# A two-layer decoder trunk on one core: first retention output weights loaded ahead of the rows, the first norm's second root moved forward, and the attention items placed three products later

## The chip, the cores and the metric

One NeuronCore of a Trainium2 chip runs the whole program. The metric is the device time of one execution in microseconds (us). TensorE does the matrix products; VectorE (DVE), ScalarE (ACT) and GpSimd (POOL) prepare its operands and take its results out of PSUM; SyncE (SP) issues nearly all transfers. The engines run their own instruction streams in a fixed order and meet at semaphores only.

## What is computed

The trunk has two pre-norm layers on 1024 tokens of width 1024, in float32. Layer 0 mixes by multi-scale retention, layer 1 by a gated linear recurrence; each is followed by a SwiGLU feed-forward part (hidden width 2816), and a last RMSNorm ends it. The change lies in the first norm and in the retention of layer 0:

```python
h = rms_norm(x, mix_norm[0])
q, k, v, g = split(h @ w_in)          # 1024, 1024, 2048, 2048 columns
q, k = rope(q), rope(k) * dk ** -0.5  # 4 heads of 256
scores = (q_i @ k_i.T) * decay        # chunk by chunk, a running state beside it
o = scores @ v_i + (q_i @ state) * q_decay
state = state * chunk_decay + (k_i * k_decay).T @ v_i
x = x + (rms(o) * silu(g)) @ w_out
```

## The kernel before, in words

**Products.** Every float32 operand is held as a high and a low part, and one product of 128x128 by 128x512 is three TensorE instructions (`three`, L1197: high by high at L1199, high by low at L1202 and L1203). The input projection runs in 24 units (`IN_ORDER`), each with a 2x2-block scheme of PRODUCTS = 7 products, so a product has a number j = 7r + p, with unit r and place p from 0 to 6; each is 4 calls of `three`, 12 instructions. Every product needs its own 128x512 weight form: ACT rounds it (L1895, in the first two units L1915), POOL takes the rest (`f_lo_of`, L927), and POOL also makes the sums of weight blocks (`f_add`, L930). ACT rounds the form of product j + 3 after product j.

**Start.** Units 0 and 1 run interleaved, while the first norm is still being made. The norm has two halves of 512 tokens. For the second half ACT and DVE square the rows, DVE sums the squares (L2543), ACT takes the root (L1822), DVE the reciprocal (L2545), both scale the rows (ACT L1987, DVE L2645), TensorE turns them (L1347), and DVE and ACT form sums and high and low parts (L2662, L2673, L1960, L1965) for the products of units 0 and 1. In ACT's program (`norm_by_halves_act`, L1949, `scaled_last`, L1990) this root stands behind four copies out of PSUM (`plain`), one weight form (`unit(3)`) and one copy of a product (`first_term`, L1923). In POOL's program (`first_units`, L961) six weight sums stand together between the fourth and the fifth weight form.

**Rotations.** Units 4, 5, 6, 7, 10, 11, 14 and 15 give q or k, which DVE rotates in twelve 128x512 operations (`turned`, L2822, at L2836): 1 and 2 at p = 4 (they read PSUM), 3 to 6 at p = 5, 7 to 9 at p = 6, 10 to 12 at p = 0 of the next unit. Operations 3 to 12 read two SBUF operands.

**Items.** The attention is cut into 16 items (4 heads by 4 pieces of 256 tokens), each with four parts that all engines put behind the same product: part 0 turns the keys and takes the scores (`keys_and_scores`, TensorE at L1578; ACT and DVE `item_keys`, with DVE's L2868, L2871, L2873), part 1 turns the values (L1598), part 2 gives outputs and state, part 3 turns the outputs back (L1632), and ACT rounds and DVE lowers the next item's q and k (ACT L2147, L2148; DVE `item_lower`, L2861, L2863). The table `PARTS` puts part m = 4 it + part behind product 47 + 16m // 9, so part 0 of item 0 is behind p = 5 of unit 6, and the last part behind p = 5 of unit 22. TensorE's part 0 waits for `item_lower` (item 0's stands behind product FIRST_PART - 1), its part 1 for DVE's `item_keys`.

**The end of the projection.** Then `out_rows` multiplies the gated rows by `w_out`: 64 weight units w, eight for the first head's rows in each half. SP's order there is: store of item 15 (L656), `load_rows(0)`, `(1)`, `(2)` (L673, two transfers of 1 MB each), the spill of unit 22 (L600, four of 256 KB), out weights 0 to 3 (L583), 4 to 7, the spill of unit 23, `load_rows(3)`. DVE gates the rows (`rows_gated`, L2903), ACT rounds them (`rows_upper`, L2194), DVE lowers them (`rows_lower`, L2907); ACT rounds the out weights (L2207) and POOL lowers them (L1143). ACT's `in_first_quarter` (L2131) of unit 23 waits for the spill of unit 22, since it writes what that spill reads.

## Time and profile before

| what | us |
|---|---|
| median of 3 runs | 2639.61 (2639.51 to 2641.33) |
| profiled execution, its own time | 2641.87 |
| its span | 2640.0 |
| TensorE busy | 2574.9 (98%) |
| GpSimd busy | 1701.5 (64%) |
| VectorE busy | 1486.8 (56%) |
| ScalarE busy | 1056.0 (40%) |
| granted TensorE clock, mean | 0.994 |

The busy time of an engine is the union of its instructions' durations. A row of the timeline gives start, duration, engine, line, operation and tiles, and in brackets how long the engine had been idle and what released it.

### The profile page before, as it was taken

The page shows a single profiled execution, that of the slowest core. Times are in us where ns is not written, and L with a number is a line of the kernel's source. Part 1 is how long each engine was busy: PE and PEld are TensorE (multiplying, and loading weights), DVE is VectorE, ACT ScalarE, POOL GpSimd, SP SyncE. Part 2 cuts the span into 40 slices and gives each one's busy share as a digit, 9 for nine tenths or more (in the row PEclk, how much of TensorE's full clock was granted, in tenths as well). Part 3 has the DMA queues.
Part 4 walks back from the last instruction along what each step waited for, and adds up shares of the span by engine and source line. Part 5 has one row for each costly group of instructions (what it writes and reads, how often), then busy time and mean ns, then how long its engine had stood idle before and what let it go on. Part 6 is the DMA issues. An engine that isn't in the chain of part 4 may idle for free.

```text
span 2640.0 us, 34384 instructions
## 1 busy us (share of the span) xinstructions
PE 2574.9 (98%) x11625; PEld 2118.0 (80%) x11625; DVE 1486.8 (56%) x1762; ACT 1056.0 (40%) x1753; POOL 1701.5 (64%) x1277
## 2 busy tenths in 40 slices
PE   6999999999999999999999999999999999999998
PEld 5778887888788788888888788888877888888887
DVE  8685647343341856556463738365688464655644
ACT  6333343555344533333333614324256333333324
POOL 5864555455565488878788645263454788887865
PEclk9999999999999999999999999999999999999999
DMA  3433533344852121121212011111111112112122
GB/s 114 138 104 115 157 120 112 112 144 145 301 191 80 49 61 52 48 60 42 61 59 64 29 49 50 39 54 40 41 56 49 48 48 64 48 48 64 48 68 84
DMA packets 250796, 214.85 MB, mean 81 GB/s; under 512 B 12481, under 2 KB 204225, under 8 KB 250689
## 3 DMA queue, kind: packets, MB, share of 16 engines
q1 hardware_dynamic: 250464, 213.40, 25.6%
q8 instruction: 62, 1.02, 0.2%
q14 instruction: 46, 0.37, 0.0%
q10 hardware_dynamic: 224, 0.07, 0.0%
HBM read 175.67 MB, written 37.75 MB: 81 GB/s over the span
## 4 chain that ended last, share of the span: by engine, by line
PE 80%; DVE 11%; issue 4%; ACT 3%; DMA 1%; POOL 1%; SPq 0%; DVEq 0%; ACTq 0%; POOLq 0%
PE ps L1199 26%; PE ps L1203 26%; PE ps L1202 26%; DVE residual L3135 2%; DVE f_h_lo L2673 1%; DVE uc L3229 1%; DVE gate_buf L2836 1%; PE ps L1347 1%; DVE uc L3223 1%; PE ps L1598 1%; DVE rope_part L2836 0%; DVE gate_buf L3234 0%; DMA projected<-gate_buf 0%; PE ps L1632 0%; DVE f_h_lo L2662 0%
## 5 line engine op out<-in xcount | busy, mean ns | idle before, releaser
L927 POOL TENSOR_TENSOR f_w_lo<-f_raw,f_w_hi 128x512 fp32r<-128x512 f32 x406 | 577.4, 1426 | 384.3 <-ACT f_w_hi L1895 221.6
L1199 PE MATMUL ps<-f_h_hi,f_w_hi 128*128 128x512 f32 x1904 | 749.4, 394 | 10.8 <-POOL f_w_lo L927 4.6
L1203 PE MATMUL ps<-f_h_hi,f_w_lo 128*128 128x512 f32 x1904 | 743.6, 391 | 0.0
L1202 PE MATMUL ps<-f_h_lo,f_w_hi 128*128 128x512 f32 x1904 | 743.0, 390 | 0.0
L1199 PEld LDWEIGHTS ps<-f_h_hi,f_w_hi 128*128 128x128 f32 x1904 | 359.0, 189 | 93.9 <-issue 9.4
L927 POOL TENSOR_TENSOR f_w_lo<-f_sum,f_w_hi 128x512 fp32r<-128x512 f32 x210 | 316.0, 1505 | 182.0 <-ACT f_w_hi L1895 181.3
L1203 PEld LDWEIGHTS ps<-f_h_hi,f_w_lo 128*128 128x128 f32 x1904 | 358.4, 188 | 75.7
L1202 PEld LDWEIGHTS ps<-f_h_lo,f_w_hi 128*128 128x128 f32 x1904 | 359.1, 189 | 71.8
L1895 ACT ACTIVATE f_w_hi<-f_raw 128x512 fp32r<-128x512 f32 x248 | 156.5, 631 | 400.6 <-PE ps L1203 396.0
L1199 PE MATMUL ps<-f_w_hi,f_act_hi 128*128 128x512 f32 x616 | 240.8, 391 | 4.5 <-DVE residual L3135 4.5
L1202 PE MATMUL ps<-f_w_lo,f_act_hi 128*128 128x512 f32 x616 | 239.8, 389 | 0.0
L1203 PE MATMUL ps<-f_w_hi,f_act_lo 128*128 128x512 f32 x616 | 239.7, 389 | 0.0
L3135 DVE TENSOR_TENSOR residual<-ps,residual 128x512 f32<-128x512 f32 x316 | 205.6, 684 | 54.4 <-PE ps L1203 54.4
L1895 ACT ACTIVATE f_w_hi<-f_sum 128x512 fp32r<-128x512 f32 x186 | 117.1, 630 | 234.0 <-PE ps L1203 230.1
L3023 DVE TENSOR_TENSOR gate_buf<-ps,gate_buf 128x512 f32<-128x512 f32 x120 | 82.9, 691 | 210.4 <-PE ps L1203 210.3
L900 POOL TENSOR_TENSOR small<-w_raw 128x1 f32<-128x1 f32 x72 | 26.2, 364 | 242.5 <-PE ps L1199 242.5
L930 POOL TENSOR_TENSOR f_sum<-f_sum,f_raw 128x512 f32<-128x512 f32 x124 | 182.0, 1468 | 0.0
L1143 POOL TENSOR_TENSOR ret_out_lo<-f_raw,ret_out_hi 128x512 fp32r<-128x512 f32 x64 | 101.8, 1595 | 84.5 <-ACT ret_out_hi L2207 84.5
L1199 PE MATMUL ps<-h_hi,w_hi 128*128 128x512 f32 x384 | 151.3, 394 | 1.0 <-DVE h_lo L2565 0.6
L1203 PE MATMUL ps<-h_hi,w_lo 128*128 128x512 f32 x384 | 149.5, 389 | 0.0
L1202 PE MATMUL ps<-h_lo,w_hi 128*128 128x512 f32 x384 | 149.5, 389 | 0.0
L1199 PEld LDWEIGHTS ps<-f_w_hi,f_act_hi 128*128 128x128 f32 x616 | 115.6, 188 | 32.4 <-DVE residual L3135 8.2
(343 smaller groups left out, 4564.7 us busy)
## 6 DMA issues: line engine op xcount, KB each, us to landing
f_raw<-in_ffn_w_gu SPq DMA_DIRECT2D x176, 256.0 KB, 3.6
f_raw<-in_ret_w_in SPq DMA_DIRECT2D x96, 256.0 KB, 5.0
projected<-gate_buf SPq DMA_DIRECT2D x96, 256.0 KB, 4.2
f_raw<-in_ffn_w_down SPq DMA_DIRECT2D x88, 256.0 KB, 2.8
f_raw<-in_ret_w_out SPq DMA_DIRECT2D x64, 256.0 KB, 3.3
w_raw<-in_lru_w_in SPq DMA_DIRECT2D x48, 256.0 KB, 2.9
residual<-in_x SPq DMA_DIRECT2D x16, 512.0 KB, 6.9
v_raw<-projected SPq DMA_DIRECT2D x16, 512.0 KB, 3.8
```

Of the source, the lines that this page charges most:

```text
L927: nc.gpsimd.tensor_tensor(lo, src, hi.bitcast(F32), ALU.subtract).then_inc(f_wready, 1)
L930: nc.gpsimd.tensor_tensor(out, one, other, op).then_inc(f_summed, 1)
L1143: nc.gpsimd.tensor_tensor(lo_, f_in_raw(w % 8), hi.bitcast(F32), ALU.subtract).then_inc(f_wready, 1)
L1199: m = nc.tensor.matmul(o, l_hi, r_hi, start=start, stop=False, skip_group_check=onto)
L1202: nc.tensor.matmul(o, l_hi, r_lo, start=False, stop=False, skip_group_check=onto)
L1203: return nc.tensor.matmul(o, l_lo, r_hi, start=False, stop=stop, skip_group_check=onto)
L1347: m = nc.tensor.transpose(ps[:, b * BANK + s * P:b * BANK + (s + 1) * P], xn_at(half, hf * 4 + s)[:, k * P:(k + 1) * P], ident[:])
L1598: m = nc.tensor.transpose(bank(4 + blk, d * P, P), v_raw[:, d * ITEM + blk * P:d * ITEM + (blk + 1) * P], ident[:])
L1895: nc.scalar.activation(f_unit(j)[0], src, ACT.Copy).then_inc(f_whi, 1)
L2673: TT(H_lo[:, h_cut(form, k)], src[:, t_cut(k)], H_hi[:, h_cut(form, k)].bitcast(F32), ALU.subtract).then_inc(hn_dve, 1)
L3023: TT(t, f_bank(u, p), t, ALU.add).then_inc(f_ev, 1)
L3135: TT(X[:, c], ps[:, b * BANK:(b + 1) * BANK], X[:, c], ALU.add).then_inc(f_ev, 1)
```

## The change

There are four parts; the diff keeps every changed line.

1. **Transfers at the end of the projection.** SP loads out weights 0 to 3 ahead of `load_rows(0)`; `load_rows(1)` follows the spill of unit 22, and `load_rows(2)` the spill of unit 23. DVE gates rows 0 at p = 2 of unit 23 and lowers them at p = 4, ACT rounds them at p = 3 and rounds out weights 0 and 1 ahead of its copy at p = 4. Rows 1 are gated, rounded and lowered only in the output stage, ahead of out weight 4.
2. **First norm.** ACT does one of the four copies ahead of the second root, `unit(3)` between root and scaling, and `first_term` and the other three copies between the two halves of the scaling. DVE makes three low parts (L2662) ahead of four squares.
3. **POOL's first sums.** The six sums are spread between the weight forms in pairs, two of them ahead of the fourth form.
4. **Items.** Part m goes behind product 50 + 7m // 4. This puts the parts 0, 1, 2, 3 behind p = 1, 2, 4, 6 of every unit from 7 to 22. Rotation operations 5 and 6 stand behind an item's part at p = 5, where there is one.

```diff
 ITEM_PARTS = 4
-FIRST_PART = 47
+FIRST_PART = 50
 PARTS = {}
 for m in range(ITEM_PARTS * ITEMS):
-    PARTS.setdefault(FIRST_PART + m * 16 // 9, []).append((m // ITEM_PARTS, m % ITEM_PARTS))
+    PARTS.setdefault(FIRST_PART + m * 7 // 4, []).append((m // ITEM_PARTS, m % ITEM_PARTS))
 def chunks_before(it):
...
 ROWS_IN = (0, 1, 2, 0, 1, 0, 1, 0)
-ROWS_AT = {8: 2, 14: 3, 20: 4, 24: 5, 28: 6, 35: 7}
+ROWS_AT = {4: 1, 8: 2, 14: 3, 20: 4, 24: 5, 28: 6, 35: 7}
 END_0 = counts(1, GROUPS_OF_4[0])
...
 SUMS_FIRST = [(0, 1), (0, 2), (0, 3), (1, 1), (1, 2), (1, 3), (0, 6), (1, 6)]
+SUMS_RET = [(u, p) for p in (1, 2, 3, 6) for u in range(2)]
...
+def first_sums(n, u, p):
...
+    return n.sums + (SUMS_RET if n == NOTHING else SUMS_FIRST).index((u, p)) + 1
...
                         if r == IN_UNITS - 2 and p == 6:
-                            load_rows(0)
-                            load_rows(1)
-                            load_rows(2)
-                        if r == IN_UNITS - 1 and p == 3:
                             for w in range(4):
                                 out_weight(w)
+                            load_rows(0)
+                        if r == IN_UNITS - 1 and p == 3:
+                            load_rows(1)
                 for w in range(4, 8):
...
                 spill(IN_UNITS - 1)
+                load_rows(2)
                 load_rows(3)
...
                     if w in (18, 24, 30, 33):
...
                 n = FIRST[layer]
-                units, sums = n.units, n.sums
+                units = n.units
                 raws = [[f_in_raw(4 * u + i) for i in range(4)] for u in range(2)]
                 def landed(u, i):
...
                 def summed(u, p):
-                    pool.wait_ge(f_summed, sums + SUMS_FIRST.index((u, p)) + 1)
+                    pool.wait_ge(f_summed, first_sums(n, u, p))
...
                     landed(u, 1)
...
                     lower(0, 4, raws[0][3])
+                    sum_1(0)
+                    sum_1(1)
                     landed(1, 3)
                     lower(1, 4, raws[1][3])
-                    for u in range(2):
-                        sum_1(u)
-                        sum_3(u)
-                        sum_2(u)
-                    sum_4(0)
                     lower(0, 1, f_in_sum(0))
                     lower(1, 1, f_in_sum(1))
-                    sum_4(1)
+                    sum_3(0)
+                    sum_3(1)
                     lower(0, 2, raws[0][1])
                     lower(1, 2, raws[1][1])
-                    summed(0, 3)
+                    sum_2(0)
+                    sum_2(1)
                     lower(0, 3, raws[0][0])
-                    summed(1, 3)
                     lower(1, 3, raws[1][0])
+                    sum_4(0)
+                    sum_4(1)
                     lower(0, 5, raws[0][2])
...
                     lower(0, 6, raws[0][3])
...
                 else:
-                    act.wait_ge(f_summed, n.sums + SUMS_FIRST.index((u, p)) + 1)
+                    act.wait_ge(f_summed, first_sums(n, u, p))
                 src = f_in_sum(u) if p == 1 else f_in_raw(slot)
...
-                def scaled_last():
+                def scaled_last(amid=lambda half: None):
                     root(4, SB, turn_b)
+                    amid(0)
                     act.wait_ge(n_rstd, turn_b)
                     for half in range(2):
+                        if half:
+                            amid(1)
                         scaled(6, half)
...
                         square_rows(s, 0, t_b[:, t_cut(s - 4)])
-                    for k in FOUR:
-                        plain(4 + k)
-                    unit(3)
-                    first_term(c, 1, AT_FIRST)
-                    scaled_last()
+                    plain(4)
...
+                    def between(half):
+                        if half == 0:
+                            unit(3)
+                        else:
+                            first_term(c, 1, AT_FIRST)
+                            for k in (1, 2, 3):
+                                plain(4 + k)
+                    scaled_last(between)
+                    unit(4)
                     act.wait_ge(n_sq, SB)
...
                     q_12(0)
...
                 from_sum(H_T1, 3, t_a, "T1")
-                unit(4)
+                if layer != RET:
+                    unit(4)
                 q_12(3)
...
                 for k in FOUR:
...
                             turn_table(p - 2, (sin_t, cos_t)[p - 2])
+                        if j == PROJECTED - 3:
+                            out_round(0)
+                            out_round(1)
                         if p == 4 and kind in "vg":
...
                         if p == 5 and kind == "g":
...
                                     item_rounded(it + 1)
-                        if r == IN_UNITS - 1:
-                            if p == 3:
-                                rows_upper(0)
-                            elif p == 4:
-                                out_round(0)
-                                out_round(1)
-                            elif p == 5:
-                                rows_upper(1)
+                        if j == PROJECTED - 4:
+                            rows_upper(0)
                 out_round(2)
             def out_ahead(end, done=[3]):
...
                         plain(H_Q11, k, k, "Q11h")
+                    for k in (0, 1, 2):
+                        plain(H_Q21, k, 4 + k, "Q21h")
                     square(5)
...
                     square(7)
-                    for k in FOUR:
-                        plain(H_Q21, k, 4 + k, "Q21h")
+                    plain(H_Q21, 3, 7, "Q21h")
                 else:
...
                         adds(0, 0)
...
                     dve.wait_ge(f_mm, PRODUCTS * r + 5)
-                elif first == 2:
+                elif first < 6:
                     dve.wait_ge(f_ev, in_ev(r, E_C21))
...
                     dve.wait_ge(f_ev, in_ev(r, E_C12))
...
                             if turn:
-                                turned(r, 2, 6)
+                                turned(r, 2, 4)
                         elif p == 6:
...
                         turn_arguments(r, p)
...
                                 item_lower(it + 1)
+                        if p == 5 and turn:
+                            turned(r, 4, 6)
                         if p == 6 and turn:
...
                         if r == IN_UNITS - 1:
-                            if p in (2, 3):
-                                rows_gated(p - 2)
-                            elif p == 5:
+                            if p == 2:
+                                rows_gated(0)
+                            elif p == 4:
                                 rows_lower(0)
-                rows_lower(1)
             def out_rows():
-                for q in range(2, 7):
+                for q in range(1, 7):
                     rows_gated(q)
...
                 for nh in range(2):
```

## Rows read from the trace of the kernel before

**Rows 1.** Page, busy time of TensorE (us, share, instructions)

```profile
PE 2574.9 (98%) x11625; PEld 2118.0 (80%) x11625; DVE 1486.8 (56%) x1762; ACT 1056.0 (40%) x1753; POOL 1701.5 (64%) x1277
```

**Rows 2.** TensorE's waits: total us, times, longest us

```profile
PE ps L1598 <- DVE item_kt_lo L2871: 4.3, 2, 2.2
...
PE ps L1578 <- DVE item_k_lo L2863: 4.3, 2, 3.3
...
PE ps L1199 <- DVE item_k_lo L2863: 1.0, 1, 1.0
```

**Rows 3.** Stretches: busy us of each engine, clock, DMA share, GB/s

```profile
26.40:66.00 39.60, 32.92 (x143) 25.88 (x142) 37.10 (x48) 24.77 (x45) 27.82 (x19) 0.91 0.04 10
...
168.00:182.00 14.00, 10.68 (x46) 9.09 (x45) 8.64 (x12) 4.55 (x8) 5.67 (x5) 0.76 0.61 185
...
661.00:666.00 5.00, 5.00 (x24) 4.14 (x23) 2.14 (x1) 0.00 (x0) 0.00 (x0) 1.00 1.05 390
```

**Rows 4.** Timeline of ACT, first norm

```profile
24.53 2.47 ACT L1960 ACTIVATE gate_buf<-ps,cols 128x512 f32<-128x512 f32 x4
...
27.81 0.38 ACT L1822 ACTIVATE rstd<-ssq,small 128x4 f32<-128x4 f32 x1
```

**Rows 5.** Timeline of DVE, first norm

```profile
25.11 0.15 DVE L2543 TENSOR_TENSOR ssq<-ssq 128x4 f32<-128x4 f32 x1
...
33.38 2.71 DVE L2662 SCALAR_TENSOR_TENSOR h_sum_a<-ps,cols,h_q 128x512 f32<-128x512 f32 x4
```

**Rows 6.** Timeline of TensorE, first norm

```profile
30.87 0.30 PE L1347 MATMUL ps<-ident,f_xn 128*128 128x128 f32 x1 [3.67 <-DVE f_xn L2645]
...
41.24 0.50 PE L1199 MATMUL ps<-f_h_hi,f_w_hi 128*128 128x512 f32 x1 [2.33 <-POOL f_w_lo L927]
```

**Rows 7.** Timeline of TensorE, items

```profile
172.37 0.45 PE L1578 MATMUL ps<-ident,k_raw 128*128 128x128 f32 x1 [3.32 <-DVE item_k_lo L2863]
...
209.82 0.45 PE L1598 MATMUL ps<-ident,v_raw 128*128 128x128 f32 x1 [2.15 <-DVE item_kt_lo L2871]
...
294.31 0.60 PE L1578 MATMUL ps<-ident,k_raw 128*128 128x128 f32 x4
...
296.13 0.40 PE L1199 MATMUL ps<-f_h_hi,f_w_hi 128*128 128x512 f32 x1
...
301.60 0.60 PE L1598 MATMUL ps<-ident,v_raw 128*128 128x128 f32 x4
```

**Rows 8.** Timeline of DVE, unit 5's rotation (no item in it), and one of POOL beside it

```profile
149.57 0.69 DVE L2806 TENSOR_TENSOR gate_buf<-gate_buf,ps 128x512 f32<-128x512 f32 x1 [1.33 <-PE ps L1203]
...
150.29 1.82 DVE L2836 TENSOR_TENSOR rope_part<-gate_buf,sin 128x512 f32<-128x512 f32 x1
...
157.14 0.68 DVE L2806 TENSOR_TENSOR gate_buf<-gate_buf,ps 128x512 f32<-128x512 f32 x1
...
158.84 1.77 DVE L2836 TENSOR_TENSOR gate_buf<-gate_buf,sin 128x512 f32<-128x512 f32 x1
...
161.13 0.68 DVE L2836 TENSOR_TENSOR gate_buf<-gate_buf,cos 128x512 f32<-128x512 f32 x1
...
150.28 1.29 POOL L927 TENSOR_TENSOR f_w_lo<-f_sum,f_w_hi 128x512 fp32r<-128x512 f32 x1 [0.17 <-ACT f_w_hi L1895]
```

**Rows 9.** Timeline of TensorE, first out weight

```profile
672.81 0.79 PE L1199 MATMUL ps<-ret_out_hi,rows_hi 128*128 128x512 f32 x1 [6.28 <-POOL ret_out_lo L1143]
```

**Rows 10.** Timeline of ACT and SP, end of the projection

```profile
658.94 1.91 ACT L2194 ACTIVATE rows_hi<-rows_o 128x2048 fp32r<-128x2048 f32 x1
...
668.69 0.60 ACT L2131 ACTIVATE gate_buf<-ps 128x512 f32<-128x512 f32 x1 [7.84 <-DMA projected<-gate_buf]
...
646.04 0.37 SPq L656 DMA_DIRECT2D attended<-o_raw  x1
```

**Rows 11.** Timeline of DVE, end of the projection

```profile
656.29 2.28 DVE L2903 TENSOR_TENSOR rows_o<-rows_o,rows_g 128x2048 f32<-128x2048 f32 x1
...
669.34 2.29 DVE L2907 TENSOR_TENSOR rows_lo<-rows_o,rows_hi 128x2048 fp32r<-128x2048 f32 x1
```

## The prediction

> **What bounds the kernel now.** I read the page first: TensorE is busy for 2574.9 of 2640.0 us [rows 1], so a gain can only be idle time of TensorE, 65 us, or time at its lower clock. Next, TensorE's waits [rows 2]: the reader should see that two of DVE's item steps, L2863 and L2871, hold it for 9.6 us. The timeline then places the waits. There are three places that the change touches: the first norm (idle 3.67 us ahead of 30.87 and 2.33 us ahead of 41.24 [rows 6]), the items (3.32 and 2.15 us [rows 7], one of 2.2 and two of 1.0, the rest of [rows 2]), and the first out weight (6.28 us [rows 9]). Last the stretches, for the clock: 0.91 in 26.4 to 66 and 0.76 in 168 to 182 [rows 3], a mean over the two levels of 1.2 and 2.4 GHz. In 168 to 182 the time lost is 14 x 0.24 = 3.4 us, of which I take 3.1 as lost by work. The second part of the idle time thus costs nearly as much as the first.
>
> **Sizes used below.** Two products fill the time from 296.13 to 301.60, so one is 2.73 us; part 0 of an item is 296.13 - 294.31 = 1.82 us [rows 7]. Parts 1 and 3, eight turns each, are two such sets of four, some 0.85 us each (0.6 us pipelined for four [rows 7]).
>
> **Part 1, the end of the projection: 7.3 us gained.** What is late now is a transfer. After the store of item 15 at 646.04 [rows 10] SP issues 6 MB of rows and then the 1 MB spill of unit 22; with the 0.5 MB store that is 7.86 million bytes, at 390 GB/s [rows 3] 20.2 us and some 2 us of latency: 668.2. The trace has ACT's copy behind that spill at 668.69, after 7.84 us of waiting [rows 10], and the out weights are rounded behind the copy. TensorE starts at 672.81 [rows 9]. In the new order I count from E, the end of the last product. Item 15 ends one product later, behind (22, 6), so its store goes out at about E - 17.4 (seven products are 19.1 us; ACT's copies follow the turns by some 1.7). Ahead of rows 0 there are then 0.5 + 1 MB, and 2 MB are theirs: 3.67 million bytes, 9.4 + 2 us, E - 6. DVE gates them in 2.28 us [rows 11] to E - 3.7, ACT rounds them in 1.91 us [rows 10] to E - 1.8, then two out weights (0.6 each) to E - 0.6. The spill has landed at E - 3.3 and is no longer waited for. DVE lowers the rows in 2.29 us [rows 11] to E + 0.6. So 0.6 us of idle time is left, up to 1.5 where a DVE operation meets one of POOL's; I take 1.0. Gone are 5.3 us of idle time, and the low clock behind it: 672.81 began at half speed, for which I take 2.0 us (4.3 us at half speed costs about 2). Moved past on SP: rows 1 now land at E + 1 or 2 with 6.5 MB ahead, needed through out weight 8 at E + 22; out weight 8 has 12.75 MB ahead of it, 34.3 us, and lands at E + 19, covered by out weights 0 to 7. Without that cover it would cost 1 to 3 us. Bounds: 4.3 gained (rows_gated and rows_lower each 1.1 longer, the spill late) to 8.3.
>
> **Parts 2 and 3, the first norm: 4.3 us gained.** The root stands at 27.81, while its sum is there at 25.26 [rows 4, 5]. With one copy ahead (four take 2.47 us, from 24.53 [rows 4]) ACT is free at 25.15, and the root is at 25.35: 2.5 us earlier. DVE's three low parts are only moved ahead of the squares: the same number stands ahead of the sum. The first set of turns follows, but the last three copies are now behind the first half of the scaling, and DVE's first sum waits for the last copy: I get 29.9 in place of 33.38 [rows 5], by seven operations of 0.6 (a weight form, two scalings, `first_term`, three copies) from 25.7 on. That is 3.5 us, and from there DVE is the bound, busy for 37.10 of 39.60 us [rows 3]. POOL's spread sums free its port in 33 to 38, where they double the length of DVE's operations; it gives 2 us to DVE and takes over half back later, since two sums then stand ahead of the weights of products (0, 3) and (1, 3). I take 0.8 of it. Lower bound 2.5 (the root alone); upper 7.5, which is the idle time of [rows 6] with half of the clock's 3.6 us. Unit 2's weights are loaded behind these, so the gain is carried on.
>
> **Part 4, the items: 8.0 us lost.** The title says three products later, and the count is 50 + 7m // 4: part 0 always behind p = 1. There is never a part at p = 5, so moving rotations 5 and 6 changes no order at all: it costs nothing and gives nothing. What counts is how much of DVE's work stands between the product (r, 5), time 0, and the part that TensorE wants. Unit 5 shows it without an item [rows 8]: operation 3 at 0.72, C12 (the third combination) at 7.57, operation 8 at 9.27, operation 10 at 11.56. An operation with two SBUF operands takes 1.7 us from start to start beside POOL and 0.6 without (operations 3 and 10: 1.82 and 0.68 long).
> - *Item 0.* `item_lower(0)` now stands behind operations 3 to 9 of unit 6, so its two steps start at 11.56 and end at 12.8; POOL is idle by then, as TensorE is held. TensorE wants them after three products, at 8.2. It idles for 4.7 us where it idled for 3.32 [rows 7]. With the same 3.1 us of clock that is 7.8 against 6.4.
> - *Units 7, 10, 11, 14, 15,* rotated with the next item behind. To TensorE's part 0 there are 2.73 x 3 + 0.85 = 9.1 us; to its part 1, 13.6. DVE has C21, operations 3 to 6, C12, two lowering steps, operations 7 to 12, one sum, the mask and the keys' low part: 10.5 us alone. Up to 7.57 the rows show four operations met by POOL (4 x 1.1 = 4.4 us), and after it I take one partly (0.4) and one fully (1.1): 16.4. So TensorE idles for 2.8 us each time, in two pieces, 14.0 in all. With none met by POOL it would be 0, with all of them 5.
> - *Gone:* 6.4 (item 0), 2.15 [rows 7] with an estimated 1.5 of clock (between none and the 3.1 of item 0), 2.2 and two of 1.0 [rows 2]: 14.3 in all.
> Loss: 7.8 + 14.0 + 0.5 for clock - 14.3 = 8.0. The other ten units have no rotation, and their lowering steps end by 8.3, ahead of 9.1.
>
> One rule is weighed here. [Rows 8] give 1.7 us for the operation that meets POOL, a cost of 1.1 over its 0.6, and I use that. The Trainium skill, page "SBUF — State Buffer", section "Who interferes with whom", says that a DVE instruction with two SBUF inputs and a GpSimd instruction that reads SBUF take the shared port in turn, and that the one that comes second is blocked for the whole of the other. By that rule each of the 5.4 meetings of a unit would cost a whole POOL instruction, 1.29 us [rows 8], 0.19 more, and the sum would be 5 us later, near 2641.
>
> **Sum.** -7.3 - 4.3 + 8.0 = -3.6 us. Against the profiled execution (2641.87 with 1.87 around its span of 2640.0) that gives 2638.3; the median of the runs is 2.3 lower, and I put the sum against it: 2639.6 - 3.6 = 2636.0.
>
> **Rivals.**
> - *The rotations collide less, clearly faster.* POOL's forms follow ACT, and ACT stands behind item work in half of these units; where POOL pauses, operations 5 and 6 fall to 0.6 us. With 1.2 us per unit in place of 2.8, part 4 costs nothing, and the time is 2628. For it: in units with an item at p = 5 these two operations do run at 0.6. Against it: that pause came from the item being there, and now there is none. With gains of part 1 and 2 at their upper ends it is 2627.
> - *DVE becomes the bound at the items, slower.* One mechanism: the lowering steps and the keys' low part come 5 us late in all five units (every operation met by POOL), 25 us in place of 14, each pause long enough to drop the clock as at 172.37. Then part 4 costs 19 us and more, and the sum is 2647. It decides from 4.6 us per unit. Against it: POOL has six instructions in that time, not ten.
> - *The transfers hold the first out weight as before.* If rows 0 were not in by E - 2, part 1 gives 3 and not 7: 2640, no change.
>
> **How the numbers follow.** A measurement of this kernel can tell about 0.2% (5.3 us) from no change: faster is below 2634.3, slower above 2644.9. The forecast, with part 4 between 6 and 13 us, has 0.35, the third rival (with the rule's 2641) 0.08: no change 0.43. The first rival has 0.30, and the upper ends of parts 1 to 3 with my part 4 have 0.12: faster 0.42, high because the sum stands only 1.7 us from that bound. The second rival has 0.15. The range takes in the first rival and goes four fifths of the way from the forecast to the second: 2627 to 2645.
>
> **What would show it.** Right: the root at about 25.4, DVE's first sum at 30, the first out weight within 2 us of the last product, a wait of some 4.7 us for L2863 at the first item, and waits for L2863 and L2871 in the units after 7, 10, 11, 14 and 15. Wrong: TensorE's waits for L2863 and L2871 below 12 us in total (then it is faster), or above 25 us (slower), or ACT still waiting for the spill ahead of L2131.

## The result, and the profile after

The changed kernel takes 2644.45 us (median of 17 runs, 2641.12 to 2648.64), the kernel before 2640.31 in the same comparison (17 runs, 2638.66 to 2642.68). The ratio is 1.0016, 95% interval 1.0010 to 1.0023: 4.2 us slower, between 2.6 and 6.1. That is within the 0.2% called "no change" in the prediction, and just inside its range, but it lies on the other side of 2639.6 than the 2636.0 forecast. The profiled execution took 2644.24, with a span of 2642.4.

TensorE's waits in the changed kernel (total us, times, longest), the rows that answer to [rows 2]:

```profile
PE ps L1585 <- DVE item_k_lo L2878: 10.4, 6, 4.8
...
PE ps L1605 <- DVE item_kt_lo L2886: 8.1, 5, 1.6
...
PE ps L1206 <- POOL ret_out_lo L1150: 3.8, 2, 3.5
```

The reader is to see 18.5 us of item waits where there were 9.6, and 3.5 ahead of the first out weight where there were 6.28 [rows 9]. Lines are shifted by some 7 in PE's part and some 15 in DVE's: L1585 is the old L1578, L2878 the old L2863. The timeline of TensorE places them; its first row answers to the first of [rows 7], its last to [rows 9]:

```profile
181.39 1.08 PE L1585 MATMUL ps<-ident,k_raw 128*128 128x128 f32 x4 [4.84 <-DVE item_k_lo L2878]
...
212.21 0.63 PE L1585 MATMUL ps<-ident,k_raw 128*128 128x128 f32 x4 [1.11 <-DVE item_k_lo L2878]
...
218.56 1.06 PE L1605 MATMUL ps<-ident,v_raw 128*128 128x128 f32 x8 [1.61 <-DVE item_kt_lo L2886]
...
675.92 0.50 PE L1206 MATMUL ps<-ret_out_hi,rows_hi 128*128 128x512 f32 x1 [3.48 <-POOL ret_out_lo L1150]
```

The pair 1.11 + 1.61 = 2.72 us stands five times, for the rotations of units 7, 10, 11, 14 and 15. The last product of the projection ends at 672.44 (666.53 before), so the first out weight stands 3.1 us later than before in all.

In the first norm, these rows of ACT and DVE answer to [rows 4, 5]:

```profile
26.28 0.30 ACT L1829 ACTIVATE rstd<-ssq,small 128x4 f32<-128x4 f32 x1 [0.76 <-DVE ssq L2557]
```

```profile
26.10 0.15 DVE L2557 TENSOR_TENSOR ssq<-ssq 128x4 f32<-128x4 f32 x1
...
30.57 2.73 DVE L2676 SCALAR_TENSOR_TENSOR h_sum_a<-ps,cols,h_q 128x512 f32<-128x512 f32 x4 [0.98 <-ACT gate_buf L1967]
...
46.08 6.80 DVE L2687 TENSOR_TENSOR f_h_lo<-h_sum_a,f_h_hi 128x512 fp32r<-128x512 f32 x4
...
53.47 2.81 DVE L2701 TENSOR_TENSOR h_sum_a<-h_sum_a,gate_buf 128x512 f32<-128x512 f32 x2
...
61.14 0.69 DVE L2687 TENSOR_TENSOR f_h_lo<-h_sum_a,f_h_hi 128x512 fp32r<-128x512 f32 x1 [0.17 <-ACT f_h_hi L1972]
```

The root is 1.5 us sooner and DVE's first sum 2.8, but four lowering steps then take 6.80 us, where four undisturbed ones take 2.48 (n1_old_sums, below). The last lowering step stands at 61.14; before it stood at 61.61.

From the two traces alone I would have said: end of the projection 3.3 us gained, first norm 0.6 gained, items 6.5 lost. The runs below show that this reading was wrong in the first and the third of its numbers.

### The profile page after: what moved, and what is told of

Its sections match the earlier page's. It is cut to its first block, busy times and chain, and to the rows that moved or that the text cites. A ratio compares the mean times of both kernels' runs of the same rounds, so it can differ in the third digit from the quotient of the medians.

```text
span 2642.4 us, 34392 instructions
## 1 busy us (share of the span) xinstructions
PE 2572.7 (97%) x11625; PEld 2115.4 (80%) x11625; DVE 1483.3 (56%) x1762; ACT 1059.2 (40%) x1755; POOL 1696.1 (64%) x1277
## 4 chain that ended last, share of the span: by engine, by line
PE 78%; DVE 12%; issue 4%; ACT 3%; POOL 1%; DMA 1%; SPq 0%; DVEq 0%; ACTq 0%; POOLq 0%
PE ps L1206 26%; PE ps L1210 25%; PE ps L1209 25%; DVE residual L3151 2%; DVE gate_buf L2851 1%; DVE f_h_lo L2687 1%; DVE uc L3245 1%; DVE rope_part L2851 1%; PE ps L1605 1%; DVE uc L3239 1%; DVE f_h_lo L2676 1%; PE ps L1354 0%; DVE gate_buf L3250 0%; POOL f_w_lo L934 0%; DVE gate_buf L2821 0%
```

## The experiments

In every one the time is given as the ratio to the kernel before, with its 95% interval.

### Each part alone

**i1_items** has the items and rotations of the change and nothing else:

```diff
-FIRST_PART = 47
+FIRST_PART = 50
-    PARTS.setdefault(FIRST_PART + m * 16 // 9, []).append(...)
+    PARTS.setdefault(FIRST_PART + m * 7 // 4, []).append(...)
...
```

> The kernel before with the items and rotations of the change alone. Theory (DVE's rotation operations ahead of the next item's lowering steps hold TensorE): a wait of 4.8 us for the first item's keys, then 1.1 + 1.6 us in each of units 7, 10, 11, 14 and 15; the last projected product ends 6.5 us later, ratio near 1.0025. Rival (the items cost nothing by themselves, the time comes from their meeting with the moved end of the projection or the moved first norm): DVE's waits stay at 9.6 us in total and the time within 1.5 us of the kernel before.

Measured: 1.0051 (1.0034 to 1.0068), 13.5 us slower, twice the theory's 6.5. The item waits are those of the changed kernel (10.3 and 8.1 us). What is new is the gap behind the last product:

```profile
PE ps L1199 <- POOL ret_out_lo L1143: 10.6, 2, 10.3
...
PE ps L1578 <- DVE item_k_lo L2863: 10.3, 6, 4.8
...
PE ps L1598 <- DVE item_kt_lo L2871: 8.1, 5, 1.6
```

Here the last product ends at 675.40 and item 15's store is issued at 658.18, 17.2 us ahead of it. In the kernel before the store stands 20.5 us ahead (646.04 [rows 10], end at 666.53). The items cost 8.8 us more of waits, and another 4.0 us at the end, since all the transfers of that stage follow the store. That makes 12.8 of the 13.5 us (interval 9.0 to 18.0).

**t1_end** has the new end of the projection and nothing else:

```diff
+                            for w in range(4):
+                                out_weight(w)
                             load_rows(0)
-                            load_rows(1)
-                            load_rows(2)
                         if r == IN_UNITS - 1 and p == 3:
-                            for w in range(4):
-                                out_weight(w)
+                            load_rows(1)
...
+                load_rows(2)
                 load_rows(3)
...
```

> The kernel before with the new end of the projection alone (out weights ahead of the rows, rows gated and rounded in the new order). Theory: TensorE's idle time ahead of the first out weight falls from 6.28 to about 3.5 us, the same low clock behind it; 3.3 us faster. Rival: the item's store goes out one product sooner than in the changed kernel, the rows are in time, and idle time falls to 1 us; 7 us faster, as predicted blind.

Measured: 0.9976 (0.9966 to 0.9985), 6.3 us faster (7.0 by the medians). The rival was right; its number, 7, lies inside the interval of 4.0 to 9.0:

```profile
666.53 0.50 PE L1199 MATMUL ps<-ret_out_hi,rows_hi 128*128 128x512 f32 x1 [0.28 <-POOL ret_out_lo L1143]
```

The idle time is 0.28 us, and the low clock that followed the long pause in both other kernels is not there: in the 5 us from the first out weight on the granted clock is 1.00 here, 0.66 in the changed kernel, and 0.50 in the kernel before (672 to 677 us). The chain of this stage has the same length in both orders of the items. Here the store is issued at 645.75 and the first out weight multiplied at 666.53, 20.78 us later; in the changed kernel 655.19 and 675.92, 20.73 us. So the changed kernel's 3.48 us are this chain of 20.7 us less the 17.2 us that the store has.

**n3_norm** has the first norm and GpSimd's new order and nothing else (parts 2 and 3 of the change, as in its diff).

> The kernel before with the new first norm and GpSimd's new order alone. Theory: the root 1.5 us earlier, DVE's first sum near 30.6, its third lowering near 42.4, and all but 0.6 us of it given back by 61 us; 0.6 us faster. Rival: the gain of 4 us is there and it is the items behind that lose it; then the last product of the projection ends 4 us earlier than in the kernel before.

Measured: 0.9994 (0.9984 to 1.0003), 1.6 us faster and not told from zero. In its trace the root stands at 25.44 and DVE's first sum at 29.73, the last lowering step of the stage is at 60.27, and the last product ends 4.1 us earlier than in the kernel before. That is the rival's number, and more than the runs of the whole kernel show (at most 4.2 by the interval, 1.6 in the middle). Much of it is clock and not work: between 168 and 182 us the granted clock is 0.88 here and 0.76 before, between 205 and 219 us 1.00 and 0.88, up to 3.4 us in all, though the item waits ahead of these are no shorter here than there (3.72 and 2.13 us against 3.32 and 2.15). The same program's stage moves from kernel to kernel: the last lowering step stands at 60.4 to 62.9 in the six kernels whose first norm is the old one, as one or two of DVE's first squares meet GpSimd at 14 to 17 us. One profile does not give this stage to better than 1 or 2 us.

**a0_old_items** is the changed kernel with the items undone:

```diff
-FIRST_PART = 50
+FIRST_PART = 47
-    PARTS.setdefault(FIRST_PART + m * 7 // 4, []).append(...)
+    PARTS.setdefault(FIRST_PART + m * 16 // 9, []).append(...)
```

> The changed kernel with the items and rotations as they were before (its first norm and its end of the projection stay). Theory (the three parts add up: 7.0 us gained at the end, 1.4 in the first norm, 13.3 lost by the items): 8.4 us faster than the kernel before, near 2632. Waits for item_k_lo and item_kt_lo fall back to some 4.6 and 4.3 us, idle time ahead of the first out weight to 0.3. Rival (something of the first norm or of the end costs time only when they are together): no more than 5 us faster than before.

Measured: 0.9968 (0.9955 to 0.9981), 8.4 us faster. The parts add up as far as their intervals tell: -6.3 - 1.6 + 13.5 = +5.6 against +4.2 measured, and without the items -7.9 against -8.4. Idle time ahead of the first out weight is 0.15 us.

### Why the items wait

**f2_late_rotation** moves rotation operations out of the item's way in i1_items:

```diff
-                        if p == 5 and turn:
-                            turned(r, 4, 6)
                         if p == 6 and turn:
-                            turned(r, 6, 9)
-                        if p == 0 and IN_ORDER[r - 1][0] in "qk":
+                            turned(r, 4, 6)
+                            turned(r, 6, 8)
+                        if p == 1 and IN_ORDER[r - 1][0] in "qk":
+                            turned(r - 1, 8, 9)
                             turned(r - 1, 9, 12)
```

> The kernel i1_items with rotation operations 5 to 8 issued behind the next item's lowering steps, and 9 to 12 behind the item's keys, and nothing else. Theory: it is these operations, each 1.1 us too long beside GpSimd, that make the lowering steps late, so the waits of 2.7 us in five units fall to 0.5 us or less, that of the first item to about 3.5; 13 us faster than i1_items and 6 us faster than the kernel before. Rival: the lowering steps wait for ScalarE's rounding of the rotated rows, or the delayed rotations hold their spills and the next unit: waits of over 2 us per unit stay or appear for another releaser.

Measured: 0.9990 (0.9980 to 1.0000), 2.6 us faster than before, which is barely told from zero, and 16 us faster than i1_items. The wait for the lowered keys is left once, at the first item (4.4 us); that of L2871 is 0.5 us in each of the five units, where it was 1.6. The lowering steps were late because of the rotation operations ahead of them: of 18.4 us of item waits 6.9 are left. Of the 16 us 12.1 are idle time (these waits, and 0.6 at the first out weight). Against the kernel before it gained less than the 6 us expected. The gap behind the last product (9.7 us) stayed, as the store still stands 17.2 us ahead of it.

**c1_late_rotation_end** is f2_late_rotation with the new end, as in t1_end.

> The kernel f2_late_rotation with the new end of the projection. Theory (the chain from the last item's store to the first out weight has a fixed length of 20.7 us, and the store stands 17.2 us ahead of the last product): idle time ahead of the first out weight 3.5 us in place of 9.7, some 9 us faster than the kernel before. Rival (the chain's length was set by DVE, which is less behind here, or by the item waits): the idle time falls to under 1 us, 12 us faster.

Measured: 0.9961 (0.9946 to 0.9976), 10.3 us faster. Store at 643.77, first out weight at 664.69, 20.9 us later; idle time 3.70 us. With most of the item waits gone, the length of the chain is still the same: it is set by what follows the store, and the cost of the items there is the place of the last item, not the waits on the way.

**p47_items_ahead_of_rotation** begins the items at p = 5, in t1_end:

```diff
 FIRST_PART = 47
-    PARTS.setdefault(FIRST_PART + m * 16 // 9, []).append(...)
+    PARTS.setdefault(FIRST_PART + m * 7 // 4, []).append(...)
...
-                            if turn:
-                                turned(r, 2, 6)
...
+                        if p == 5 and turn:
+                            turned(r, 2, 6)
                         if p == 6 and turn:
```

> The kernel t1_end (items as in the kernel before, new end of the projection) with the change's spacing of the items, seven products each, but begun at product 47 and with rotation operations 3 to 6 behind the item's keys, so that the next item's lowering steps (behind product 3) and the keys (behind product 5) both stand ahead of the rotation operations. Theory (it is the place of the item's DVE work in the rotated unit that costs, not the spacing): of DVE's item waits only that of the first item stays, 3.5 us, against 8.8 in t1_end; the last store goes out two products sooner, so no idle time ahead of the first out weight; 5 to 6 us faster than t1_end, 12 to 13 faster than the kernel before. Rival (the items' rows come too late for a sooner start, or the held rotation makes the next unit late): new waits at the first products of an item, no faster than t1_end.

Measured: 0.9937 (0.9920 to 0.9953), 16.6 us faster than before, some 10 more than t1_end. The first six of TensorE's waits in this kernel:

```profile
PE ps L1671 <- DMA vec<-in_lru_lambda: 9.7, 1, 9.7
PE ps L1199 <- POOL f_w_lo L927: 4.7, 3, 2.4
PE ps L1199 <- DVE residual L3131: 4.5, 9, 0.5
PE ps L1347 <- DVE f_xn L2642: 4.2, 2, 3.7
PE ps L1199 <- DVE f_h_lo L2670: 3.8, 6, 0.8
PE ps L1578 <- DVE item_k_lo L2860: 3.7, 1, 3.7
```

The wait for item_kt_lo is gone and that for item_k_lo is left once. The spacing of seven products is the same as in the change: what counts is where in the unit the item's DVE work falls. The gain is 4 us more than I expected of it, which its interval (12.4 to 21.1) does not tell from the 12 to 13 expected. Of the 10 us over t1_end the item waits account for 6.1 (9.8 there, with one of 1.0 at L1199, and 3.7 here). Another part is clock: between 168 and 182 us the granted clock is 0.88 here and 0.76 in t1_end, between 205 and 219 us 1.00 and 0.88, up to 3.4 us in all.

### The first norm

**n1_old_sums** has ACT's and DVE's new order, and GpSimd's sums as before (the change's part 2 without part 3).

> The kernel before with the new order of ScalarE and DVE in the first norm, and GpSimd's sums in their old order. Theory (the time that DVE loses to GpSimd in this stage is some 7 us wherever the sums stand): the root sooner by 1.5 to 2 us, DVE's scalings 4.8 to 5.0 us long for the four in place of 2.8, the last lowering step within 1 us of n3_norm, 0 to 1.5 us faster than before. Rival (the spread sums are what gives the old gain back): 3 us faster than before.

Measured: 0.9986 (0.9976 to 0.9995), 3.7 us faster. That is the rival's number. Its interval (1.3 to 6.3 us) overlaps that of n3_norm (0.8 slower to 4.2 faster), so the times alone do not tell the two apart; the traces do. The last lowering step stands at 57.30 here and at 57.18 in b_best, which has the same first norm, and at 60.27 to 61.14 in the four kernels with the spread sums and the new order (n3_norm, the changed one, a0_old_items, a3_split_lowering). ACT, DVE and POOL in n1_old_sums, and below them in n3_norm:

```profile
23.96 0.30 ACT L1822 ACTIVATE rstd<-ssq,small 128x4 f32<-128x4 f32 x1
```

```profile
10.44 1.68 DVE L2655 TENSOR_SCALAR gate_buf<-residual,rstd 128x512 f32<-128x512 f32 x4
...
24.50 4.83 DVE L2655 TENSOR_SCALAR f_xn<-residual,rstd 128x512 f32<-128x512 f32 x4
...
31.89 2.36 DVE L2683 TENSOR_TENSOR f_h_lo<-h_sum_a,f_h_hi 128x512 fp32r<-128x512 f32 x2
...
34.84 2.76 DVE L2683 TENSOR_TENSOR f_h_lo<-h_sum_a,f_h_hi 128x512 fp32r<-128x512 f32 x2
...
46.52 2.48 DVE L2683 TENSOR_TENSOR f_h_lo<-h_sum_a,f_h_hi 128x512 fp32r<-128x512 f32 x4
...
57.30 0.69 DVE L2683 TENSOR_TENSOR f_h_lo<-h_sum_a,f_h_hi 128x512 fp32r<-128x512 f32 x1 [0.17 <-ACT f_h_hi L1965]
```

```profile
46.91 4.96 POOL L927 TENSOR_TENSOR f_w_lo<-f_raw,f_w_hi 128x512 fp32r<-128x512 f32 x2 [0.47 <-ACT f_w_hi L1915]
```

```profile
25.44 0.30 ACT L1829 ACTIVATE rstd<-ssq,small 128x4 f32<-128x4 f32 x1 [0.93 <-DVE ssq L2560]
```

```profile
21.66 1.78 DVE L2657 SCALAR_TENSOR_TENSOR h_sum_b<-residual 128x512 f32<-128x512 f32 x1
...
25.99 2.77 DVE L2662 TENSOR_SCALAR f_xn<-residual,rstd 128x512 f32<-128x512 f32 x4
29.73 2.73 DVE L2679 SCALAR_TENSOR_TENSOR h_sum_a<-ps,cols,h_q 128x512 f32<-128x512 f32 x4 [0.97 <-ACT gate_buf L1967]
...
45.22 6.80 DVE L2690 TENSOR_TENSOR f_h_lo<-h_sum_a,f_h_hi 128x512 fp32r<-128x512 f32 x4
...
60.27 0.69 DVE L2690 TENSOR_TENSOR f_h_lo<-h_sum_a,f_h_hi 128x512 fp32r<-128x512 f32 x1 [0.17 <-ACT f_h_hi L1972]
```

```profile
45.10 3.00 POOL L937 TENSOR_TENSOR f_raw<-f_sum,f_raw 128x512 f32<-128x512 f32 x2
```

With the sums in their old place the four scalings of DVE take 4.83 us and not 2.77, but DVE then finds ACT ready, and the four steps later are undisturbed. They are so although GpSimd begins a form at 46.91, inside them: there GpSimd is the one that waits, its two forms take 4.96 us and not 2.5. With the sums spread, DVE saves 2.1 us at 26 and 2.3 at 32 to 37, waits 0.97 of it for ACT's copy, and pays 4.3 at 45, where a sum of GpSimd's is already running (from 45.10) when its four steps begin (45.22). It has also paid 1.1 at 21.66, where a square meets one of the sums that now stand ahead of the fourth form (GpSimd's starts at 21.58); the root hangs on that square, and stands at 25.44 in place of 23.96. The reader can add it up in one number: the time by which DVE's operations with SBUF operands alone, up to the last lowering step, are longer than undisturbed ones (0.60 us each, and 0.40 for a scaling, as the four at 10.44 show). It is 8.9 us in n1_old_sums and 10.5 in n3_norm.

**f1_sums_early** puts the sums where GpSimd waits:

```diff
+                    sum_3(0)
+                    sum_3(1)
                     lower(0, 1, f_in_sum(0))
+                    sum_2(0)
+                    sum_2(1)
                     lower(1, 1, f_in_sum(1))
-                    sum_3(0)
-                    sum_3(1)
+                    sum_4(0)
+                    sum_4(1)
                     lower(0, 2, raws[0][1])
...
```

> The kernel n3_norm with GpSimd's third and second sums right behind its weights of products (0, 4), (1, 4) and (0, 1), where it waits, and its fourth ahead of the weights of product (0, 2). Theory (the sums stood beside DVE's lowering steps at 46 to 56 us, where ScalarE and the weights waited for them): DVE's four lowering steps of 46.1 take 2.5 to 3.5 us in place of 6.8, ScalarE's wait of 3.0 for f_raw goes, some 3 us faster than n3_norm and 4 faster than before. Rival (the sums cost DVE the same wherever they meet it, now at 33 to 41): within 1 us of n3_norm.

Measured: 1.0000 (0.9990 to 1.0009), 1.6 us slower than n3_norm by the ratios, not told from equal. DVE in this kernel:

```profile
26.13 4.80 DVE L2662 TENSOR_SCALAR f_xn<-residual,rstd 128x512 f32<-128x512 f32 x4
...
33.48 2.95 DVE L2690 TENSOR_TENSOR f_h_lo<-h_sum_a,f_h_hi 128x512 fp32r<-128x512 f32 x2
...
37.02 3.27 DVE L2690 TENSOR_TENSOR f_h_lo<-h_sum_a,f_h_hi 128x512 fp32r<-128x512 f32 x2
...
49.21 5.73 DVE L2690 TENSOR_TENSOR f_h_lo<-h_sum_a,f_h_hi 128x512 fp32r<-128x512 f32 x4
```

ACT's wait for f_raw is gone, as expected, but DVE now loses time at 26, at 33 and at 37, where the sums are, and still at 49, where GpSimd has three weight forms in a row (46.50 to 52.09). The same sum of lost time is 12.2 us. My theory that ACT's wait was the cost was wrong: it is gone and nothing is gained. The time that DVE loses fits, to within what the runs tell apart.

**n0_sums_cut** leaves work out of n3_norm: six of the eight sums of the first two units run on 8 columns, so the weights of products (u, 2), (u, 3) and (u, 6) are not the reference's.

```diff
-                    f_add(raws[u][1], raws[u][0], raws[u][1], ALU.subtract)
+                    f_add(raws[u][1][:, 0:8], raws[u][0][:, 0:8], raws[u][1][:, 0:8], ALU.subtract)
```

> The kernel n3_norm with six of GpSimd's eight sums of the first pair of units done on 8 of their 512 columns, so that the weights of products (u, 2), (u, 3) and (u, 6) are not the reference's. Theory (each sum that meets one of DVE's operations with two SBUF inputs costs DVE its own length or nearly so): DVE's four steps of 6.8 us at 45 fall to some 4 us, those of 2.8 and 1.8 at 52.6 and 55.3 to 1.3 and 1.2, the last lowering step stands 3 to 4 us earlier, 3 us faster than n3_norm. Rival (DVE is held by the lowering forms of the weights or by ScalarE, and the sums cost nothing): within 1 us of n3_norm.

```profile
46.12 4.86 DVE L2690 TENSOR_TENSOR f_h_lo<-h_sum_a,f_h_hi 128x512 fp32r<-128x512 f32 x4
...
51.55 2.05 DVE L2704 TENSOR_TENSOR h_sum_a<-h_sum_a,gate_buf 128x512 f32<-128x512 f32 x2
...
57.63 0.69 DVE L2690 TENSOR_TENSOR f_h_lo<-h_sum_a,f_h_hi 128x512 fp32r<-128x512 f32 x1 [0.17 <-ACT f_h_hi L1972]
```

The last lowering step stands 2.6 us earlier than in n3_norm though the root is 0.9 later, and the lost time is 7.3 us. The remaining 2.4 us at 46.12 stand mostly beside weight forms. The ratio is 0.9952 (0.9936 to 0.9969), 12.7 us faster. That is more than this stage can give: the first out weight is only 1.65 us earlier than in n3_norm, so over 8 us come later, with other data in all later stages. I use only the rows of the first norm from this run.

### The lock at the first out weight

DVE and POOL in the changed kernel, end of the projection:

```profile
668.16 2.29 DVE L2918 TENSOR_TENSOR rows_o<-rows_o,rows_g 128x2048 f32<-128x2048 f32 x1 [5.87 <-DMA rows_g<-projected]
...
672.44 2.29 DVE L2922 TENSOR_TENSOR rows_lo<-rows_o,rows_hi 128x2048 fp32r<-128x2048 f32 x1 [1.38 <-ACT rows_hi L2211]
```

```profile
673.00 7.40 POOL L1150 TENSOR_TENSOR ret_out_lo<-f_raw,ret_out_hi 128x512 fp32r<-128x512 f32 x3 [6.68 <-ACT ret_out_hi L2224]
```

POOL's first form begins at 673.00, beside DVE's step, which ends at 674.73; TensorE begins at 675.92, 1.2 us later, about the length of one form alone (1.29 [rows 8]). **a3_split_lowering** cuts DVE's step in four:

```diff
+                if q == 0:
+                    for c in range(3):
+                        s = slice(512 * c, 512 * c + 512)
+                        TT(rows_lo[0][:, s], o_and_g(0)[0][:, s], rows_hi[0][:, s].bitcast(F32), ALU.subtract)
...
```

> The changed kernel with the 128x2048 lowering step of the first rows as four steps of 128x512. Theory (GpSimd's first form of an out weight, begun beside it, stands still for the whole of the DVE instruction that has the port): GpSimd gets in after a piece of 0.6 us, the idle time ahead of the first out weight falls from 3.5 to 1.8 to 2.5 us, 1 to 1.7 us faster than the changed kernel. Rival (the two share the port evenly, or the out weight isn't what is last): the idle time stays at 3.5 us.

Measured: 1.0016 (1.0006 to 1.0026), the same as the changed kernel. DVE, POOL and TensorE in this kernel:

```profile
671.79 4.04 DVE L2925 TENSOR_TENSOR rows_lo<-rows_o,rows_hi 128x512 fp32r<-128x512 f32 x3 [1.38 <-ACT rows_hi L2211]
675.75 0.68 DVE L2927 TENSOR_TENSOR rows_lo<-rows_o,rows_hi 128x512 fp32r<-128x512 f32 x1
```

```profile
672.35 2.93 POOL L1150 TENSOR_TENSOR ret_out_lo<-f_raw,ret_out_hi 128x512 fp32r<-128x512 f32 x2 [6.72 <-ACT ret_out_hi L2224]
```

```profile
676.53 0.76 PE L1206 MATMUL ps<-ret_out_hi,rows_hi 128*128 128x512 f32 x1 [4.78 <-DVE rows_lo L2927]
```

As the theory has it, POOL gets in after the first piece and has two forms in 2.93 us. But DVE pays for them, its four pieces end at 676.4, and TensorE waits 4.78 us for DVE in place of 3.48 for POOL, where 1.8 to 2.5 were expected. The first product needs DVE's whole step and POOL's first form, so it waits for both, whoever has the port first; here POOL's second form, which it does not need, gets in between as well.

### The parts that gained, together

**b_best** is p47_items_ahead_of_rotation with the first norm of n1_old_sums.

> The parts that gained, together: the kernel p47_items_ahead_of_rotation with the first norm of n1_old_sums (ScalarE's and DVE's new order, GpSimd's sums in their old order). Theory (the parts lie in stages that don't overlap, so they add up): 16.6 + 3.8 us, 20 us faster than the kernel before, near 2620. Rival (what the first norm gives is taken back by the item's first wait, which hangs on a later chain): within 1 us of p47_items_ahead_of_rotation, near 2624.

Measured: 0.9926 (0.9912 to 0.9940), 2618.01 us (median of 5 runs), 19.5 us faster than the kernel before (15.8 to 23.2) and some 24 faster than the changed one. Over p47_items_ahead_of_rotation that is 2.9 us by the ratios, as the theory had it, but the intervals do not tell it from the rival.

## Why the prediction was right or wrong

- **Part 1, the end of the projection (7.3 us gained).** As an edit it was sized right: alone it gives 6.3 (interval 4.0 to 9.0), with 0.28 us of idle time left and no low clock, and behind the later items it gives as much (c1_late_rotation_end is 7.7 us faster than f2_late_rotation by the ratios, 6.2 by the medians). The step that failed is the chain behind the later store of the changed items: rows 0 landing at E - 6 and, from that, "0.6 us of idle time is left". I made the chain from the store to the first out weight 18.0 us, 18.4 with the allowance that I took; it is 20.7. Two terms were too short. I counted bytes at 390 GB/s from the store on. But at first the transfers are slower, as the stretches show (DMA share and GB/s are the last columns):

```profile
656.00:660.00 4.00, 4.00 (x19) 3.34 (x18) 0.69 (x1) 1.75 (x3) 1.63 (x2) 1.00 0.90 255
658.00:663.00 5.00, 5.00 (x24) 4.14 (x23) 1.38 (x2) 1.26 (x2) 2.62 (x3) 1.00 0.91 285
663.00:668.00 5.00, 5.00 (x24) 4.14 (x23) 0.00 (x0) 0.63 (x1) 1.89 (x2) 1.00 1.05 401
```

  The store is issued at 655.19, and nothing moves before 656. Between 656 and 660 us the DMA engines are busy for 0.90 of the time and yet move only 255 GB/s; why their packets are slower there no run shows. Rows 0 are issued 3.1 us behind the store, as SP needs 2.48 us for the four out weights now ahead; since the DMA engines had work meanwhile, it is not shown that this costs anything. Rows 0 are in 13.0 us behind the store, where I had 11.4. The second term is POOL's form behind DVE's step: from there to the first out weight it is 7.8 us, where I had 6.6. I had allowed "up to 1.5 where a DVE operation meets one of POOL's"; it met a whole 128x2048 step, of which 1.7 us were left.
- **Parts 2 and 3, the first norm (4.3 us gained).** Alone they give 1.6. What was forecast up to 30 us came: the root was put at 25.35 and DVE's first sum at 29.9, and n3_norm has 25.44 and 29.73; the changed kernel has 26.28 and 30.57, since one more of the first squares met GpSimd there. The step that failed is the sign of part 3, "I take 0.8 of it" for POOL's spread sums. Part 2 by itself gives 3.7 (n1_old_sums), where the prediction had 3.5 for it; part 3 takes 2.1 back by the ratios, and 3.0 at the last lowering step (57.30 against 60.27). The reason I gave for a later cost, two sums ahead of the weights of (0, 3) and (1, 3), stands in the trace (ACT waits 3.01 us for f_raw at 47.35), but f1_sums_early removes that wait and gains nothing. What was not seen is that a sum ahead of the fourth form meets a square ahead of the root, that a freed DVE at 27 us runs into a wait for ACT (0.98 us), and that at 45 a sum is under way when DVE's four steps begin, so that DVE waits for GpSimd at each of them (6.80 us), where in n1_old_sums a form that begins inside them waits for DVE (2.48 us).
- **Part 4, the items (8.0 us lost).** The mechanism and the waits were right within 0.15 us: 4.7 forecast and 4.84 measured at item 0, 2.8 and 2.72 in each of five units, in two pieces, and the split of operations 5 and 6 changes no order of the program, though no run has it alone. f2_late_rotation shows the cause as the prediction put it. The size was off: alone the items cost 13.5 us (9.0 to 18.0). Missing was a term. I charged the later store to part 1 only, where I thought it covered. It costs 4.0 us of idle time in i1_items and 3.3 in the changed kernel (3.48 against 0.15 in a0_old_items), and behind the 3.48 us the granted clock is low (0.66 in the next 5 us, where t1_end has 1.00).
- **The sum.** With the runs' numbers it is -6.3 - 1.6 + 13.5 = +5.6, and +4.2 was measured; the forecast was -3.6. Of the error 5.5 us lie in the items with what hangs on their store, 2.7 in the first norm and 1.0 in the end; these numbers have intervals of 1 to 4 us to either side, so their sum of 9.2 agrees with the 7.8 that it has to explain.
- **The rivals.** The third, the transfers holding the first out weight, came nearest, though for the items' sake and only in part; I gave it 0.08. Its condition was not met: rows 0 were in 4.3 us ahead of the last product's end, where I had 6 and the rival less than 2, and POOL's form did the rest. The rotations did not collide less, and DVE did not reach 4.6 us per unit. Two side sums of mine do not come out, and neither enters the forecast: the upper bound of parts 2 and 3 is 6.0 + 1.8 = 7.8 by its own terms, not 7.5, and the upper ends of parts 1 to 3 with part 4 at nothing give 2624, not 2627.
- **The rule that was weighed.** The item waits came out at 2.72 us per unit. With the 1.1 us per meeting of the rows I had 2.8; with a whole POOL instruction, 1.29, it would be 3.8. At the first out weight the trace agrees with what the Trainium skill, page "SBUF — State Buffer", section "Who interferes with whom", says of a whole instruction being waited for: POOL's form stood from 673.00 to DVE's end at 674.73, and its result was there 1.2 us after that. There the whole rest of a long instruction counts; for operations of 0.6 us the measured 1.1 was the better price.

## What to carry to other kernels

When a step is moved later in a program, ask at once for its last instance: what hangs on it at the end of the stage, and how long that chain is from its issue to its use, with the transfers' rate as it is at their start (255 GB/s here, and 401 only 7 us later). Two edits that are each sized right can share one slack, so size them together, and run each alone afterwards, since the difference of two traces put 6.5 us on an edit that costs 13.5 (9.0 to 18.0) alone. Where two engines share a port, moving one's work beside another's idle time helps only if the time the other wins is used; count the lost time over the whole stage, not at the place that looks worst. And before a difference of two traces is put down to an edit, compare the granted clock of the same stretches: it was worth up to 3.4 us between kernels whose waits there are alike.

## What was unexpected of the hardware

- A 128x512 form of POOL takes 1.29 us alone, and 2.9 us when it begins beside a 128x2048 step of DVE that has 1.7 us left. Cut in four, the same step took 4.6 us from first start to last end in place of 2.29, with POOL's two forms in 2.93, and the kernel was no faster.
- Three kernels with the new order in the first norm rank by the sum of DVE's lost time: 8.9, 10.5 and 12.2 us went with -3.7, -1.6 and 0.0 us against the kernel before. Their intervals overlap, and the kernel before, whose root is 2.2 to 3.9 us later, has 10.6, so the sum is no measure across different orders.
- Four 128x512 steps of DVE took 2.48 us where a form of GpSimd began inside them (46.91, n1_old_sums), and 6.80 us where a sum of GpSimd's had begun 0.12 us ahead of them (45.10, n3_norm).
- A pause of 2.13 us of TensorE ahead of the same step (an item's values, at 209.47 and 207.24) was followed by the lower clock in t1_end (0.88 between 205 and 219 us) and not in n3_norm (1.00).
- The same instructions of the first norm end up to 2.5 us apart in kernels that differ only far behind it (last lowering step at 60.4 to 62.9), with one or two meetings of DVE's first squares and GpSimd's forms at 14 to 17 us.
